# Modulation rows as products of upper and lower parts ahead of the first product and beside the scan, and step sizes in two and four tiles

## What is computed

```python
mod_l = (jax.nn.silu(c) @ w_mod[i] + b_mod[i])[:, None, :]
mod_c = (jax.nn.silu(c_ctx) @ w_mod[i] + b_mod[i])[None, None, :]
sh1_l, sc1_l, g1_l, sh2_l, sc2_l, g2_l = jnp.split(mod_l, 6, axis=-1)
p_l = modulate(rmsnorm(h_lat, norm1[i]), sh1_l, sc1_l) @ w_in[i]
p_c = modulate(rmsnorm(h_ctx, norm1[i]), sh1_c, sc1_c) @ w_in[i]
z_l, xs_l, b_l, c_l, dtf_l, dtb_l = ssd_inputs(p_l, ssd_conv_w[i], ...)
y_c, s_f, s_b = ssd_bidir(xs_c, b_c, c_c, dtf_c, dtb_c, a_f, a_b, h0, h0)
y_l, _, _ = ssd_bidir(xs_l, b_l, c_l, dtf_l, dtb_l, a_f, a_b, s_f, s_b)
```

## Time and profile before

| | us |
|---|---|
| median of 3 runs | 4663.7 (4660.9 to 4664.33) |
| profiled execution, its time | 4673.91 |
| its span, first to last instruction | 4672.1 |
| PE busy | 4511.7 (97%) |
| DVE busy | 2590.9 (55%) |
| ACT busy | 1572.2 (34%) |
| POOL busy | 1473.3 (32%) |

### The profile page before, as it was taken

One profiled execution on the slowest core, in us unless ns is written; L12 is line 12 of the kernel. 1 busy time (PEld: TensorE's weight loads), 2 busy tenths in 40 slices (PEclk: granted clock), 3 DMA queues, 4 the chain that ended last, 5 costly groups with the idle time before them and its releaser, 6 DMA issues.

```text
span 4672.1 us, 55907 instructions
## 1 busy us (share of the span) xinstructions
PE 4511.7 (97%) x22503; PEld 3755.4 (80%) x22503; DVE 2590.9 (55%) x3684; ACT 1572.2 (34%) x2168; POOL 1473.3 (32%) x961
## 2 busy tenths in 40 slices
PE   7999999999999999999999999999999999999998
PEld 4757845879889999999888767788788778887887
DVE  4856667469779987888522345322322455444223
ACT  3334211233335543333322344322322332123222
POOL 2032024206877657777310201210210201112101
PEclk8999999999999999999999999999999998899999
DMA  4142412225766699999422221222222221001222
GB/s 173 50 152 93 147 54 79 75 82 194 258 226 233 251 354 385 373 387 387 180 95 95 82 74 53 78 94 95 86 95 95 101 83 41 23 33 64 95 93 75
DMA packets 228969, 663.48 MB, mean 142 GB/s; under 512 B 22167, under 2 KB 87975, under 8 KB 226536
## 3 DMA queue, kind: packets, MB, share of 16 engines
q1 hardware_dynamic: 112832, 398.15, 24.3%
q0 software_dynamic: 38752, 143.03, 8.4%
q10 hardware_dynamic: 77128, 118.73, 7.0%
HBM read 591.66 MB, written 68.16 MB: 141 GB/s over the span
## 4 chain that ended last, share of the span: by engine, by line
PE 83%; DVE 11%; POOL 2%; ACT 2%; issue 1%; DMA 1%; DVEq 0%; ACTq 0%; POOLq 0%; SPq 0%
PE ps L257 20%; PE ps L258 20%; PE ps L259 20%; PE ps L1536 2%; DVE r L226 2%; DVE A L1965 2%; PE ps L584 2%; PE ps L1615 1%; DVE A L2264 1%; PE ps L3368 1%; PE ps L3375 1%; DVE A L2265 1%; PE ps L268 1%; PE ps L3352 1%; PE ps L389 1%
## 5 line engine op out<-in xcount | busy, mean ns | idle before, releaser
L257 PE MATMUL ps<-r,r 128*128 128x512 f32 (+2 forms) x5160 | 1932.0, 374 | 20.1 <-POOL r L226 14.6
L258 PE MATMUL ps<-r,r 128*128 128x512 f32 (+2 forms) x5160 | 1914.5, 371 | 0.0
L259 PE MATMUL ps<-r,r 128*128 128x512 f32 (+2 forms) x5160 | 1913.7, 371 | 0.0
L226 DVE TENSOR_TENSOR r<-A,r 128x1024 fp32r<-128x1024 f32 x588 | 779.6, 1326 | 1430.0 <-ACT r L220 1429.9
L220 ACT ACTIVATE r<-A 128x1024 fp32r<-128x1024 f32 x665 | 704.4, 1059 | 1756.9 <-PE ps L259 1595.5
L257 PEld LDWEIGHTS ps<-r,r 128*128 128x128 f32 x5160 | 973.3, 189 | 167.7 <-issue 25.4
L258 PEld LDWEIGHTS ps<-r,r 128*128 128x128 f32 x5160 | 973.3, 189 | 136.2 <-issue 3.4
L259 PEld LDWEIGHTS ps<-r,r 128*128 128x128 f32 x5160 | 972.6, 188 | 135.3
L276 POOL TENSOR_TENSOR r<-A,r 128x512 fp32r<-128x512 f32 (+2 forms) x303 | 403.9, 1338 | 1374.4 <-ACT r L273 1239.6
L273 ACT ACTIVATE r<-A 128x512 fp32r<-128x512 f32 (+1 forms) x264 | 150.6, 579 | 418.8 <-DVE A L2338 232.3
L226 POOL TENSOR_TENSOR r<-A,r 128x1024 fp32r<-128x1024 f32 x77 | 206.7, 2686 | 160.1 <-ACT r L220 159.2
(11 more groups left out here) (508 smaller groups left out, 4680.3 us busy)
## 6 DMA issues: line engine op xcount, KB each, us to landing
A<-in_pu SPq DMA_DIRECT2D x128, 512.0 KB, 4.3
A<-in_pv SPq DMA_DIRECT2D x128, 512.0 KB, 6.7
A<-in_f1i SPq DMA_DIRECT2D x88, 512.0 KB, 3.2
A<-in_f2i SPq DMA_DIRECT2D x88, 512.0 KB, 3.2
A<-in_w_mod SPq DMA_DIRECT2D x48, 512.0 KB, 4.1
A<-in_w_in SPq DMA_DIRECT2D x48, 512.0 KB, 3.3
acts<-A ACTq DMA_DIRECT2D x128, 192.0 KB, 4.4
gates<-A ACTq DMA_DIRECT2D x8, 3072.0 KB, 11.5
```

The lines of the kernel that those rows point to most:

```text
L226: e.tensor_tensor(self.vr(at + 1024, 1024), self.v(self.st0 + 1024 * (u % RS), 1024), self.vr(at, 1024).bitcast(F32), ALU.subtract).then_i ...
L257: t.matmul(o, hi, xh, start=first and k == k0, stop=False)
L258: t.matmul(o, hi, xl, start=False, stop=False)
L259: m = t.matmul(o, lo, xh, start=False, stop=final and k == K - 1)
```

## The change

The change replaces the fp32 row product for rows 0 to 3 and 7 to 11 by products of rounded parts. The condition columns are made into four: two upper (ACT, "c upper") and two lower (DVE, "c parts"). Each k step is then one instruction with the upper part and one with the lower part of the w_mod unit, both 4 x 512 out, and the four rows of PSUM are copied, turned and summed. The units of these rows go through the ring: upper part on ACT, lower part on DVE, staging buffer free at the lower part. Units of rows 4 to 6 (w_mod 16 to 27) stay raw. The places of the parts are written anew: in `pre` one unit at a time with squares and additions between, in `states` three units at the end, in `prod` four ahead of the first decay, then one after each n for which `row_ahead` holds (n = 2 to 5, 8 to 10, 12 to 14, 16 to 18), and one at the start of o = 2, 3 and 4. Apart from it, `conv_t` makes the step sizes of two token tiles ahead of the context's product and of four behind it.

```diff
...
 RS, RW = 3, 3
-RAW = ("w_mod",)
 PRM_COLS = [
...
             if u >= RS and self.units[u - RS][0] != "pause":
-                s.wait_ge(*self.S.at("used" if self.units[u - RS][0] in RAW else "lo", u - RS))
+                s.wait_ge(*self.S.at("used" if self.raw(u - RS) else "lo", u - RS))
             s.dma_start(self.v(self.st0 + 1024 * (u % RS), 1024), self.T[name][i]).then_inc(*self.S.dma(f"st{u % RS}", "load", u))
+    def raw(self, u):
+        name, i = self.units[u]
+        return name == "w_mod" and 16 <= i < 28
     def hi(self, a, u):
-        if u < len(self.units) and self.units[u][0] not in RAW + ("pause",):
+        if u < len(self.units) and self.units[u][0] != "pause" and not self.raw(u):
             a.wait_ge(*self.S.at("load", u))
...
     def lo(self, e, who, u):
-        if u < len(self.units) and self.units[u][0] not in RAW + ("pause",) and self.lo_of[u] == who:
+        if u < len(self.units) and self.units[u][0] != "pause" and not self.raw(u) and self.lo_of[u] == who:
             at = self.wr0 + 2048 * (u % RW)
...
         self.top = L.AL + 32
+        L.SC4 = self.al(32)
         L.XR = [L.BTOK + 512 * k for k in range(6)] + [self.al(512), L.ROW]
+    def modrows(self, n):
+        return 2 if 4 <= n < 7 else 4
     def modmm_t(self, t, n, b, ks=range(8)):
...
             self.cur["t"] += 4
-            if j == 0:
-                t.wait_ge(*S.at("load", u))
-            m = t.matmul(self.PS[b][0:2, :], self.v(L.SCM + 2 * k, 2), self.v(self.st0 + 1024 * (u % RS) + 128 * j, 512), start=k == 0, stop=k == 7)
+            if self.raw(u):
+                if j == 0:
+                    t.wait_ge(*S.at("load", u))
+                m = t.matmul(self.PS[b][0:2, :], self.v(L.SCM + 2 * k, 2), self.v(self.st0 + 1024 * (u % RS) + 128 * j, 512), start=k == 0, stop=k == 7)
+            else:
+                if j == 0:
+                    t.wait_ge(*S.at("lo", u))
+                    t.wait_ge(*S.at("c parts"))
+                hi, lo = (self.vr(self.wr0 + 2048 * (u % RW) + x, 1024)[:, 128 * j:128 * j + 512] for x in (0, 1024))
+                t.matmul(self.PS[b][0:4, :], self.vr(L.SC4, 32)[:, 4 * k:4 * k + 4], hi, start=k == 0, stop=False)
+                m = t.matmul(self.PS[b][0:4, :], self.vr(L.SC4, 32)[:, 4 * k:4 * k + 4], lo, start=False, stop=k == 7)
             if j == 4 or k == ks[-1]:
...
     def modtr_t(self, t, n, b):
         S, L = self.S, self.L1
+        R = self.modrows(n)
         t.wait_ge(*S.at("modrow", n))
...
             at = L.ROW + 512 * (n % 2) + 128 * o
-            m = t.transpose(self.PS[b][:, 2 * o:2 * o + 2], self.A[0:2, at:at + 128], self.A[0:2, self.cst0:self.cst0 + 2])
+            m = t.transpose(self.PS[b][:, R * o:R * o + R], self.A[0:R, at:at + 128], self.A[0:R, self.cst0:self.cst0 + R])
         m.then_inc(*S.on("t", "modtr", n))
     def modrow_v(self, v, n, b):
         S, L = self.S, self.L1
+        R = self.modrows(n)
         v.wait_ge(*S.at("modmm", n))
...
         at = L.ROW + 512 * (n % 2)
-        v.tensor_copy(self.A[0:2, at:at + 512], self.PS[b][0:2, :]).then_inc(*S.on("v", "modrow", n))
+        v.tensor_copy(self.A[0:R, at:at + 512], self.PS[b][0:R, :]).then_inc(*S.on("v", "modrow", n))
     def modset_v(self, v, n, b):
         S = self.S
+        R = self.modrows(n)
         v.wait_ge(*S.at("modtr", n))
         m3 = self.v(self.MOD, 96).rearrange("p (a o) -> p o a", a=2)[:, 4 * n:4 * n + 4, :]
-        v.tensor_tensor(m3, self.PS[b][:, 0:8].rearrange("p (o a) -> p o a", a=2),
-                        self.prm("b_mod", 4 * n, 4).unsqueeze(2).to_broadcast([128, 4, 2]), ALU.add).then_inc(*S.on("v", "modset", n))
+        ps = self.PS[b][:, 0:4 * R].rearrange("p (o a) -> p o a", a=R)
+        bias = self.prm("b_mod", 4 * n, 4).unsqueeze(2).to_broadcast([128, 4, 2])
+        if R == 2:
+            v.tensor_tensor(m3, ps, bias, ALU.add).then_inc(*S.on("v", "modset", n))
+        else:
+            v.tensor_tensor(m3, ps[:, :, 2:4], bias, ALU.add).then_inc(*S.on("v"))
+            v.wait_ge(*S.last("v"))
+            v.tensor_tensor(m3, m3, ps[:, :, 0:2], ALU.add).then_inc(*S.on("v", "modset", n))
     def modcol_v(self, v, i, at, name):
...
                 t.wait_ge(*S.at("modrow", n - 2))
-            self.modmm_t(t, n, 2 + n % 2, range(6) if n == 3 else range(8))
+            self.modmm_t(t, n, 2 + n % 2, range(4) if n == 3 else range(8))
             if n == 2:
...
         self.modtr_t(t, 2, 4)
-        self.modmm_t(t, 3, 3, range(6, 8))
+        self.modmm_t(t, 3, 3, range(4, 8))
         t.wait_ge(*S.at("modset", 1))
...
         a.activation(self.v(L.SCM, 16).rearrange("p (k a) -> p k a", a=2), pc, ACT.Silu).then_inc(*S.on("a", "silu c"))
+        c4 = self.vr(L.SC4, 32).rearrange("p (k r) -> p k r", r=4)
+        a.wait_ge(*S.last("a"))
+        a.activation(c4[:, :, 0:2], self.v(L.SCM, 16).rearrange("p (k a) -> p k a", a=2), ACT.Copy).then_inc(*S.on("a", "c upper"))
         a.activation(self.v(L.AL, 32), self.prm("a_log", 0, 32), ACT.Exp).then_inc(*S.on("a", "a exp"))
-        a.wait_ge(*S.at("x"))
-        for k in range(8):
-            a.activation(self.v(L.SQ + 512 * k, 512), self.H(k), ACT.Square).then_inc(*S.on("a", "x sq", k))
-        a.wait_ge(*S.at("ctx"))
-        for k in range(8):
-            a.activation(self.v(L.SQ + 4096 + 256 * k, 256), self.v(L.XC + 256 * k, 256), ACT.Square).then_inc(*S.on("a", "ctx sq", k))
+        for u in range(RW):
+            self.hi(a, u)
+        for c in range(13):
+            self.weights_a(a, 8)
+            if c == 4:
+                a.wait_ge(*S.at("x"))
+            for k in range(2 * c - 8, 2 * c - 6) if 4 <= c < 8 else ():
+                a.activation(self.v(L.SQ + 512 * k, 512), self.H(k), ACT.Square).then_inc(*S.on("a", "x sq", k))
+            if c == 8:
+                a.wait_ge(*S.at("ctx"))
+            for k in range(4 * c - 32, 4 * c - 28) if 8 <= c < 10 else ():
+                a.activation(self.v(L.SQ + 4096 + 256 * k, 256), self.v(L.XC + 256 * k, 256), ACT.Square).then_inc(*S.on("a", "ctx sq", k))
         self.rstd_a(a, self.v(L.XTOK + 1024, 512), "x")
         self.rstd_a(a, self.v(L.XTOK + 2560, 256), "ctx")
-        for n in range(3):
-            self.weights_a(a, 32)
-        self.weights_a(a, 8)
         for k in range(8):
...
     def pre_v(self, v):
         S, L = self.S, self.L1
+        c4 = self.vr(L.SC4, 32).rearrange("p (k r) -> p k r", r=4)
+        v.wait_ge(*S.at("c upper"))
+        v.tensor_tensor(c4[:, :, 2:4], self.v(L.SCM, 16).rearrange("p (k a) -> p k a", a=2), c4[:, :, 0:2].bitcast(F32), ALU.subtract).then_inc(*S.on("v", "c parts"))
+        for u in range(RW):
+            self.lo(v, "v", u)
         q = self.v(L.SQ, 512)
-        for k in range(1, 8):
-            v.wait_ge(*S.at("x sq", k))
-            if k > 1:
-                v.wait_ge(*S.last("v"))
-            v.tensor_tensor(q, q, self.v(L.SQ + 512 * k, 512), ALU.add).then_inc(*S.on("v"))
-        S.mark("v", "squares", "x")
         r1, r2 = self.v(L.XTOK + 1024, 512), self.v(L.XTOK + 2560, 256)
-        for n in range(2):
-            self.modrow_v(v, n, 2 + n)
+        for c in range(12):
+            self.weights_v(v, 8)
+            if c in (3, 7):
+                self.modrow_v(v, c // 4, 2 + c // 4)
+            for k in range(max(2 * c - 8, 1), 2 * c - 6) if 4 <= c < 8 else ():
+                v.wait_ge(*S.at("x sq", k))
+                if k > 1:
+                    v.wait_ge(*S.last("v"))
+                v.tensor_tensor(q, q, self.v(L.SQ + 512 * k, 512), ALU.add).then_inc(*S.on("v"))
+            if c == 7:
+                S.mark("v", "squares", "x")
         self.rstd_v(v, 1, 512, 1.0 / 1024, 1e-6, r1, "x", 0)
...
             self.modset_v(v, n, 4 + n)
+        self.modrow_v(v, 2, 2)
+        self.weights_v(v, 8)
         self.rstd_v2(v, r1, "x")
...
         for h in range(2):
-            self.modrow_v(v, 2 + h, 2 + h)
             if h:
+                self.modrow_v(v, 3, 3)
                 self.scaled_v(v, 2, r1)
...
                     self.scaled_v(v, k, r1)
-        for n in range(3):
-            self.weights_v(v, 32)
         self.pre_lo_v(v, 0)
         self.rstd_v2(v, r2, "ctx")
-        self.weights_v(v, 24)
+        self.weights_v(v, 16)
         for k in range(3, 9):
...
             t.wait_ge(*S.at("shifted", name, 7))
-            for tt in range(4) if b == 0 else (4, 5):
+            for tt in (0, 1) if b == 0 else (2, 3, 4, 5):
                 for k in range(8):
...
     def states_v(self, v):
...
         self.after(v, "v", "conv")
-        for n in range(3):
-            self.weights_v(v, 32)
+        self.weights_v(v, 72)
         for n, (d, c) in enumerate(self.WALK):
...
                 self.modset_v(v, (n + 1) // 2, 4 + (n + 1) // 2 % 2)
+        self.weights_v(v, 24)
         self.end("v", "states")
     def scaled_tokens_a(self, a, dst, c, d, key):
...
     def states_a(self, a):
...
         self.after(a, "a", "conv")
```

(17 more changed lines are left out.)

## The result

| | median us (runs) | ratio to before, 95% interval |
|---|---|---|
| before | 4662.4 (4660.9 to 4664.3) | |
| changed | 4697.6 (4691.7 to 4705.6) | 1.0077 (1.0062 to 1.0092) |

The profiled execution of the changed kernel took 4696.2 us, its span 4694.4. In the code after, the upper part is L225, the lower part L231, the row products of parts are L600 and L601, the mask product is L1213, the minimum L1206, TensorE's products of a head L1149 and L1150, the step sizes L838.

What follows compares the result with a forecast made beforehand. TensorE, busy for 97% of the span, was taken to bound the kernel, so offsets carry to the end. First stage +9, step sizes -4 and scan +15.5 sum to +20.5 us: 4684 us on the median's scale, range 4656 to 4702.

Steps and rivals of the forecast that it cites:

- likeliest case: Whole kernel: first stage and scan lose more than the step sizes gain, 4684 us, own range 4674 to 4696; 62%.
- The sign and the carrying on: Whole kernel: slower at 70%, and offsets made in the first stage and the scan are carried to the end whole.
- The row product: TensorE's modulation rows: 16 products 0.225 us apart, 3.6 us a row instead of 7.14, so 3.5 us less each.
- The first stage: Rows 0 to 3 ahead of the first product: reciprocal at 53.6 us, first product at 63.5; +9 us, bounds +5 and +12.
- The step sizes: Two tiles ahead of the context's product, four behind: first silu at 92.8 to 94.9 us against 97.96; -4 us, bounds -8 and 0.
- the slower of the two cases: Context's product with four microseconds at the low clock: it ends 6.2 us earlier, instead of 8.2 at the high level.
- The start of the scan: Units queued ahead of the first decay: first minimum at 287.5 us, row 9's product ends at 322.1 against 309.6; +12.5 us.
- A pair of heads: Scan, DVE and ACT queue: 21.9 us for row 9 to 10 and 20.9 for row 10 to 11, against 19.6 and 18.6.
- the whole scan: Rows 7 to 11: last product of head 9 at 388.1 us against 372.6; +15.5 us, start included, bounds +5 and +20.
- the rule quoted in the prediction: Scan: DVE instructions with two SBUF inputs and GpSimd instructions reading SBUF exclude one another for a whole instruction.
- second rival: Scan: each of 13 lower parts waits for a GpSimd product, +17 us on the sum, +35 or so, 4700 us; 8%.
- Rival 1: Scan: lower parts fit into DVE's waits and TensorE stays the bound; about -18 us, 4646 us; 12%.

Runs made afterwards that it cites:

- experiment 6: Changed kernel with only rows 0 to 3 in parts, step sizes of before, root and reciprocal of x ahead of unit 15's parts: 4672.8 us, ratio 1.0028.
- experiment 4: Kernel before with rows 7 to 11 in parts, step sizes in two and four tiles, ACT's upper part ahead of the exponent: 4657.8 us, ratio 0.9988.
- experiment 9: Changed kernel with only ACT's upper part moved ahead of the exponent: 4669.5 us, ratio 1.0009 to the kernel before.
- experiment 5: Kernel before with only rows 9 to 11 in parts, upper part ahead of the exponent, step sizes in two and four tiles: 4646.8 us, ratio 0.9962.

## Why the prediction was right, and which terms were mis-sized

**The number.** The forecast was 4684 us in a range of 4656 to 4702, and 4697.6 was measured: in the range, but above the likeliest case's own 4674 to 4696. The sum was +20.5 us; the ratio's interval means +29 to +43. So the kinds of terms were right, and two of the three were too small.

**The sign and the carrying on** were right: the two stages made the loss, and it was carried to the end.

**The row product** was sized well for the high clock. TensorE's timeline of the changed kernel, four weight columns, 0.23 us apart, so 3.7 us a row where I took 3.6:

```profile
25.38 0.40 PE L600 MATMUL ps<-r,r 128*4 128x512 f32 x1
25.61 0.39 PE L601 MATMUL ps<-r,r 128*4 128x512 f32 x1
```

At the 1.2 GHz level of the first stage they start 0.43 us apart (37.52, 37.95), so at that pace a row costs 6.9 us and saves next to nothing against the 7.14 of the earlier trace rows, which the kernel before has at the high clock.

**The first stage,** +9 us: measured +10.8 (and +10.2 alone) at the end of the product of x, against the first profile of before. That profile is itself late there. The product of x ends at 68.6 to 70.9 us in the eight traces with rows 0 to 3 raw and at 80.7 to 84.2 in the five with them in parts (experiment 6 left out); the means are 12.5 us apart, at the upper bound of +12. Followed unit by unit, the additions and lower parts of units 8 to 10 came about 1 us early, and unit 14's lower part ended at 50.0 where I had 50.5. The miss is behind it: the reciprocal came at 56.0 where I had 53.6. What I missed is that unit 15's upper part waits for TensorE to use unit 12, behind sums over partitions and transpositions at the 1.2 GHz level. An estimate from rows of the same work at either level: the context's sum (1.22 us instead of 0.59), the transpositions (1.01 instead of 0.65, with four rows and not two) and unit 12's products (1.87 instead of 1.10) make some 1.8 us of those 2.4.

**The step sizes,** -4 us: this term was about right, and the first trace of the changed kernel hides it. That trace gives -8.3 (from +10.8 to +2.5), because in it the granted clock stayed high through both products and fell only at 97 us, so that four tiles took 8.25 us where I had 10.1:

```profile
81.70 3.65 PE L838 MATMUL ps<-A 128*128 128x32 f32 x32
90.96 8.25 PE L838 MATMUL ps<-A 128*128 128x32 f32 x64
```

Windows of that trace, of TensorE's matmuls alone:

```profile
86.00:88.00 2.00, 2.00 (x20) 1.00 1.03 422
...
96.00:98.00 2.00, 2.00 (x16) 0.74 0.00 0
```

In the second profile of the same kernel the clock fell inside the context's product, as in the slower of the two cases that I had worked out, and once more in the four tiles. Its timeline:

```profile
84.17 3.65 PE L838 MATMUL ps<-A 128*128 128x32 f32 x32
94.95 10.71 PE L838 MATMUL ps<-A 128*128 128x32 f32 x64
```

Its windows:

```profile
88.00:90.00 2.00, 2.00 (x12) 0.50 0.76 309
...
98.00:100.00 2.00, 2.00 (x13) 0.56 0.71 260
```

From the first step size to the first transposition, the eight traces with two and four tiles take 18.8 us (this one), 20.4, 21.4 and five times 22.1 to 22.5; the six with four and two take 25.4 to 28.7, four of them 27.1. The means are 5.6 us apart, the usual values 4.6 to 5.0. The -8.3 is the luckiest of eight.

One part of the reasoning did not hold: ACT's table load did not stand behind the step sizes. It began at 98.17 us when the convolution was done, a microsecond before the last step size (and at 102.16, with the silu at 105.70, in the second profile):

```profile
98.17 1.28 ACT L955 ACT_TABLE_LOAD   x1 [5.47 <-DVE A L919]
99.47 0.63 ACT L955 ACTIVATE A<-A 128x512 f32<-128x512 f32 x1
```

**The start of the scan.** The lower part of unit 50 was to end at 285.3 and the first minimum to start at 287.5; the trace has 286.5 and 288.31, 1.2 of which came with it, so the queue at the start was forecast well. Row 9's product ended at 327.8 instead of 322.1: the miss lies in heads 0 to 3, which took 39.5 us from the first minimum to there and not 34.6. **A pair of heads** was to take 21.9 and 20.9 us; from row copy to row copy it takes 23.8 (327.93 to 351.72) and 21.9. Within a pair, the first minima of heads 4 and 5 are 10.4 us apart (330.88 to 341.32), where I had 9. For the whole scan I had +15.5 with an upper bound of +20, and the runs give +23 to +26. This is the term that was mis-sized most. Two things were missing, and neither was in my sum of durations:

TensorE's clock. Idle for a fifth of the time, it got a mean of 0.86 between 318 and 342 us. The products of a head then take 5.8 us from first to last pair (317.17 to 322.93) instead of 3.3 (331.04 to 334.36), the row product waits behind them, and the fourth unit's upper part waits for that row product to free its buffer. I had named the clock for the first stage and the step sizes only. With the upper part out of the chain, the window 320 to 360 us reads 1.00 where it read 0.89; the changed kernel:

```profile
320.00:360.00 40.00, 34.23 (x228) 27.41 (x226) 23.00 (x46) 13.68 (x20) 16.87 (x11) 0.89 0.21 73
```

The same window of experiment 4, with more done by every engine:

```profile
320.00:360.00 40.00, 36.99 (x284) 29.86 (x282) 33.73 (x64) 20.09 (x30) 23.28 (x15) 1.00 0.31 106
```

How much of the 8 us is the clock was not measured by itself.

DVE beside GpSimd. The lower part takes 1.52 us in place of 1.23 and the mask product 1.75 in place of 0.84 where one of GpSimd's products (1.27 alone) runs:

```profile
338.37 1.82 POOL L1243 TENSOR_TENSOR A<-A 128x512 f32<-128x512 f32 x1 [2.08 <-ACT A L1165]
```

That is 0.3 + 0.9 us in a head with two units, more than the 0.35 of the earlier trace rows (that row is of head 3, not of head 5 as I wrote), and both engines' instructions lengthen. By the rule quoted in the prediction (the Trainium skill, "SBUF — State Buffer", "Who interferes with whom") the two share a port under an exclusive lock, and whoever issued first has it. The durations agree: GpSimd's product starts while DVE's lower part has 0.7 us to go and lasts 0.55 us longer; the mask product starts beside GpSimd's and lasts 0.9 us longer. No run varied this. It was my second rival as a mechanism, at a smaller price than its 17 us: in the changed kernel four mask products (1.75 us each) are 3.6 us longer in all. And the measured 4697.6 us lies nearer to that rival's 4700 than to my 4684, but experiment 4 rules it out as the cause: it has the same lengthened mask products and no loss in the scan, and TensorE waits 3.6 us for mask products there instead of 16.6.

**The scale.** I set the sum against the profiled execution and took off its 10.2 us to reach the median. That was sound for the level, but hid that this execution's excess lay behind 3850 us; the spans' difference (22.3 us) agreed with my sum (20.5) partly by that chance. Against the second profile of before, the changed kernel is at +27.6 and +35.7 us at 420 us. Added up from all traces, the three terms are 12.5, -5.6 and some +23.5, together +30.

**Rival 1** (TensorE stays the bound, 4646 us) fell for the kernel as changed. Its condition, heads under 7.6 us, is met once ACT's part leaves the chain (6.45 us in experiment 4), but its time is not: the changed kernel with that edit alone stands at 4669.5 us (experiment 9), since the first stage and the start of the scan still cost what they cost. That experiment 5 has 4646.8 us is chance; it leaves rows 0 to 3, 7 and 8 as they were.

## What to carry to other kernels

Work for an engine that is half idle is not free if its idle time lies between the links of one chain: look for the wait that the new instruction can fill on its own engine (here ACT's wait for DVE), and put it there, not behind the instruction that others wait for. A queue of prepared units ahead of a stage holds up its first instruction while the ring's loads come and go, so look at what it costs to start such a stage with nothing queued; here that, with two rows fewer in parts, was worth 10 to 12 us. Where a chain comes to idle the matrix engine, sum its work at the lower clock too. And read a term of a few us from several traces before you explain it: the first trace put the step sizes at twice their usual gain.

## What the runs showed of the hardware

The rounded product with 4 weight columns goes at the same pace as with 128 at the high clock, 0.23 us for 512 columns, so narrow weights save nothing; at the 1.2 GHz level it takes 0.43 us. In the first stage TensorE's waits for lower parts came with a granted clock of 0.50 between 37 and 45 us in all six traces that have them, and 1.00 in all eight that don't. Two executions of one kernel differ with the granted clock: two profiles of the changed kernel stand 9 us apart before the scan, and two of the kernel before 12 us behind 3850 us, with equal instructions. Instructions of DVE and GpSimd that read SBUF at the same time lengthened one another, 0.84 to 1.75 us and 1.27 to 1.82 us.
